# Two of eleven chunks of a feed forward product as seven block products, in four of five stages

## What is computed

```python
def swiglu(x, w_in, w_out):
    a, b = jnp.split(x @ w_in, 2, axis=-1)
    return (jax.nn.silu(a) * b) @ w_out

f = swiglu(rms_norm(h, g[0]), ffn1_w_in[l], ffn1_w_out[l])
h = h + FFN_RES * rms_norm(f, g[1])
...
ffn = jnp.dot(jax.nn.silu(jnp.dot(h2, w_ffn_gate)) * jnp.dot(h2, w_ffn_up), w_ffn_down)
```

## Time and profile before

| what | value |
|---|---|
| device time, median of 3 runs | 1419.55 us (1419.17 to 1420.1) |
| span of the profiled execution | 1417.5 us |
| median above that span | 2.05 us |
| PE busy | 1404.2 us, 99% |
| DVE busy | 940.8 us, 66% |
| ACT busy | 723.2 us, 51% |
| POOL busy | 150.7 us, 11% |
| weights and all else read from HBM | 280.70 MB |

### The profile page before, as it was taken

How to read it: one execution, slowest core, us unless ns; L and a number is a source line. 1 busy time by engine, 2 the same in 40 slices (tenths; PEclk the granted TensorE clock), 3 DMA queues, 4 the chain that set the end, 5 groups by cost and what they waited for, 6 DMA issues and landing times.

```text
span 1417.5 us, 19077 instructions
## 1 busy us (share of the span) xinstructions
PE 1404.2 (99%) x7339; PEld 1149.0 (81%) x7339; DVE 940.8 (66%) x1294; ACT 723.2 (51%) x1042; POOL 150.7 (11%) x232
## 2 busy tenths in 40 slices
PE   9999999999999999999999999999999999999998
PEld 7888888688888888888878888888877788888886
DVE  6666667886676667665786857755568666765544
ACT  6444455564443445543755645446556644654442
POOL 1600010010000000000172100000552110000000
PEclk9999999999999999999999999999999999999999
DMA  9686765256876778868544688763945355565551
GB/s 317 199 252 201 260 203 205 68 177 199 259 243 206 235 233 259 252 216 264 181 144 163 202 205 265 250 211 125 247 154 194 119 178 179 163 209 184 201 193 61
DMA packets 236346, 286.15 MB, mean 202 GB/s; under 512 B 37028, under 2 KB 160720, under 8 KB 236256
## 3 DMA queue, kind: packets, MB, share of 16 engines
q1 hardware_dynamic: 235856, 284.63, 63.1%
q10 hardware_dynamic: 400, 0.31, 0.1%
HBM read 280.70 MB, written 4.20 MB: 201 GB/s over the span
## 4 chain that ended last, share of the span: by engine, by line
PE 95%; DVE 2%; issue 1%; ACT 1%; DMA 0%; SPq 0%; POOL 0%; POOLq 0%; ACTq 0%
PE ps L583 30%; PE ps L586 29%; PE ps L584 29%; PE pst L790 1%; PE pst L949 1%; DVE wlo L475 1%; PE pst L1225 1%; PE ps L1172 0%; DMA raw<-in_ffn_w_in_dram 0%; ACT whi L466 0%; PE pst L1539 0%; PE pst L2112 0%; PE ps L1209 0%; PE ps L1689 0%; PE pst L2321 0%
## 5 line engine op out<-in xcount | busy, mean ns | idle before, releaser
L475 DVE TENSOR_TENSOR wlo<-raw,whi 128x1024 fp32r<-128x1024 f32 (+2 forms) x474 | 564.2, 1224 | 252.3 <-ACT whi L466 250.7
L466 ACT ACTIVATE whi<-raw 128x1024 fp32r<-128x1024 f32 (+2 forms) x474 | 472.3, 1040 | 233.7 <-PE ps L586 94.0
L583 PE MATMUL ps<-whi,xh 128*128 128x512 f32 (+2 forms) x1438 | 563.9, 392 | 1.8 <-ACT xh L829 0.8
L584 PE MATMUL ps<-wlo,xh 128*128 128x512 f32 (+2 forms) x1438 | 553.6, 385 | 0.0
L586 PE MATMUL ps<-whi,xl 128*128 128x512 f32 (+2 forms) x1438 | 545.1, 385 | 0.0
L583 PEld LDWEIGHTS ps<-whi,xh 128*128 128x128 f32 x1438 | 270.0, 188 | 61.9 <-issue 4.7
L586 PEld LDWEIGHTS ps<-whi,xl 128*128 128x128 f32 x1438 | 270.0, 188 | 54.9
L584 PEld LDWEIGHTS ps<-wlo,xh 128*128 128x128 f32 x1438 | 270.2, 188 | 51.0
L583 PE MATMUL ps<-whi,gh 128*128 128x512 f32 x440 | 172.0, 391 | 0.0
L584 PE MATMUL ps<-wlo,gh 128*128 128x512 f32 x440 | 171.2, 389 | 0.0
L586 PE MATMUL ps<-whi,gl 128*128 128x512 f32 x440 | 153.4, 389 | 0.0
(11 more groups left out here) (272 smaller groups left out, 894.2 us busy)
## 6 DMA issues: line engine op xcount, KB each, us to landing
raw<-in_ffn_w_in_dram SPq DMA_DIRECT2D x174, 512.0 KB, 5.4
raw<-in_ffn_w_out_dram SPq DMA_DIRECT2D x40, 1024.0 KB, 5.8
raw<-in_w_in_dram SPq DMA_DIRECT2D x26, 1024.0 KB, 5.1
adat<-in_w_ada_dram SPq DMA_DIRECT2D x96, 256.0 KB, 3.1
raw<-in_w_ffn_gate_dram SPq DMA_DIRECT2D x22, 512.0 KB, 4.1
raw<-in_w_ffn_up_dram SPq DMA_DIRECT2D x22, 512.0 KB, 5.1
raw<-in_hyb_w_in_dram SPq DMA_DIRECT2D x10, 1024.0 KB, 5.2
raw<-in_gla_w_in_dram SPq DMA_DIRECT2D x10, 1024.0 KB, 5.1
```

The lines of the kernel that those rows point to most:

```text
L466: e.activation(split_of(whi, j), raw_of(j), ACT.Copy).then_inc(*whi_made.up(j))
L475: e.tensor_tensor(split_of(wlo, j), raw_of(j), split_of(whi, j).bitcast(F32), ALU.subtract).then_inc(*wlo_made.up(j))
L583: e.matmul(ps[:, 0:n], a, whi_of(j, k), start=first and k == 0, stop=False)
L584: last = e.matmul(ps[:, 0:n], a, wlo_of(j, k), start=False, stop=False)
```

## The change

In stages 2, 3, 5 and 7, chunks 8 and 9 of the first product (x of 256x1024 by weights of 1024x1024: 512 columns of a and 512 of b) become one product of 2x2 blocks in Strassen's way (in Winograd's form): seven products of 128 rows by 512 by 512 columns in the place of eight. Each has one unit of weights and 12 matmuls. Sums of blocks of x are made and split once a stage (`sxh`, `sxl`). Sums of blocks of the weights are made by DMAs of POOL that add onto what lies in the buffer (`accum_op`), in `rowx` (both `rows`) and `workx` (`junk` and `xtmp`), but for one sum, which VectorE makes (`dve_t2`). P2 alone has its weights in the `raw` ring. Three results are copied out of their bank by ScalarE (`act_part`), two subtracted by VectorE (`dve_combine`). The seven stand one by one between the other chunks: 0, 1, P1, 2, P2, 3, P5, 4, P6, 5, P3, 6, P7, 7, P4, 10. Four banks are kept for them, and chunks from 2 on all use the same two banks. `ada_units` counts the products' units too: a stage has 37 units for 34. The loads of the gain vectors move to the first unit of the down product.

The core of the diff (left out: buffer declarations, the new index tables `JC`, `JP`, `JD` in the place of `J0[st] + 4 * c`, the calls of `pool_strassen(e, st)` behind the openings in POOL's program, and VectorE's loop, which mirrors ScalarE's: `dve_combine` after the fourth splits of chunks 5 and 7, `dve_sx` after the gates of chunk 1, `dve_sx_lo` after those of chunk 2, glo and the pair's gates in P4):

```diff
+    def next(self, name, *until, tile=None):
+        k = (self.n if tile is None else tile) % len(self.tiles)
+        self.n += tile is None
         self.freed = [s.at(*what) for s, *what in self.held[k]]
         self.held[k], self.place[name] = list(until), k
...
-            for c in range(11):
+        STRASSEN = (2, 3, 5, 7)
+        PAIR = 8
+        BLOCK = {"p1": ("x1", 0, 0), "p2": ("ring", 1, 0), "p5": ("x1", 0, 1), "p6": ("x1", None, None),
+                 "p3": ("x2", 1, 1), "p7": ("x2", 0, 1), "p4": ("x1", 1, 0)}
+        product_unit, home, chunk_unit, down_unit = {}, {}, {}, {}
+        def sequence(st):
+            if st in STRASSEN:
+                return (0, 1, "p1", 2, "p2", 3, "p5", 4, "p6", 5, "p3", 6, "p7", 7, "p4", 10)
+            return tuple(range(11))
...
+            if i in home:
+                return
+            s = ring_no[i] % NRAW
...
-                e.wait_ge(*(s_first.at(0) if u == 0 and k else s_raw[u % NRAW].at(u)))
+                if u not in home:
+                    e.wait_ge(*(s_first.at(0) if u == 0 and k else s_raw[ring_no[u] % NRAW].at(u)))
+                elif plan[u][0]:
+                    e.wait_ge(*(s_x1 if home[u] == "x1" else s_x2)[k // 2].at(u))
+                else:
+                    e.wait_ge(*summed.at(u, "t2"))
...
+                if j in sum_before:
+                    dve_t2(e, sum_before[j])
...
+        sum_before = {JP[st, "p6"] - 3: st for st in STRASSEN}
+        def dve_t2(e, st):
+            e.wait_ge(*wlo_made.at(last_sub[product_unit[st, "p5"]]))
+            for half in range(2):
+                e.wait_ge(*s_x2[half].at(product_unit[st, "p3"]))
+            e.tensor_tensor(rowx[:, :], rowx[:, :], workx[:, :], ALU.add).then_inc(*summed.up(product_unit[st, "p6"], "t2"))
...
+        def pool_strassen(e, st):
+            def split(name):
+                e.wait_ge(*wlo_made.at(last_sub[product_unit[st, name]]))
+            e.wait_ge(*f_scaled.at(st - 1, 1, 1))
+            pool_product(e, st, "p1", False)
+            split("p1")
+            pool_product(e, st, "p5", True)
+            e.wait_ge(*xlo_made.at(st, "sums"))
+            pool_product(e, st, "p3", False)
+            split("p6")
+            pool_product(e, st, "p4", True)
+            split("p3")
+            pool_product(e, st, "p7", True)
...
+        def dve_sx(e, st):
...
+            e.wait_ge(*squares.at(("h", st, 1), 1))
+            e.wait_ge(*xlo_made.at(st, 1, 3 if st == 7 else 1))
+            e.tensor_tensor(junk[:, :].rearrange("p (k n) -> p k n", k=8), whole(xh), whole(xl), ALU.add
+                            ).then_inc(*summed.up(st, "x", 0))
+            e.tensor_tensor(a22, a21, a22, ALU.subtract).then_inc(*summed.up(st, "x", "p5"))
+            e.wait_ge(*summed.at(st, "x", "p5"))
+            e.tensor_tensor(a21, a11, a21, ALU.subtract).then_inc(*summed.up(st, "x", "p7"))
+            e.wait_ge(*summed.at(st, "x", "p7"))
+            e.tensor_tensor(a11, a22, a11, ALU.subtract).then_inc(*summed.up(st, "x", "p6"))
+            e.wait_ge(*summed.at(st, "x", "p6"))
+            e.tensor_tensor(a12, a12, a11, ALU.add).then_inc(*summed.up(st, "x", "p3"))
+        def act_sx(e, st):
+            e.wait_ge(*summed.at(st, "x", "p3"))
+            e.activation(sxh[:, :], workx[:, :], ACT.Copy).then_inc(*xhi_made.up(st, "sums"))
+        def dve_sx_lo(e, st):
+            e.wait_ge(*xhi_made.at(st, "sums"))
+            e.tensor_tensor(sxl[:, :], workx[:, :], sxh[:, :].bitcast(F32), ALU.subtract).then_inc(*xlo_made.up(st, "sums"))
...
+        def pe_product(e, st, name, base):
+            bank, tile, first, until = {
+                "p1": ("a", 4, True, (silu_made, st, PAIR, 1)), "p2": ("b", None, False, None),
+                "p5": ("c", 5, True, (gated, st, PAIR, 1)), "p3": ("d", 3, False, (gated, st, PAIR, 0)),
+                "p6": ("a", None, False, None), "p7": ("a", None, False, None), "p4": ("a", None, False, None)}[name]
+            if tile is not None:
+                acc.next((st, bank), until, tile=base + tile)
+                for done in acc.freed:
+                    e.wait_ge(*done)
+            if name == "p1":
+                acc.next((st, "b"), (silu_made, st, PAIR, 0), tile=base + 2)
+                b_freed[st] = acc.freed
+            ps = acc.of(st, bank)
+            if name == "p5":
+                e.wait_ge(*xlo_made.at(st, "sums"))
+            if name == "p2":
+                e.wait_ge(*part_made.at(st, "p1"))
+            if name in ("p3", "p7"):
+                e.wait_ge(*summed.at(st, "c12"))
+            if name == "p4":
+                e.wait_ge(*summed.at(st, "c22"))
+            def block(z, sums, k):
+                if name in x_sums:
+                    o = x_sums[name] * 512 + k * P
+                    return sums[:, o:o + P]
+                return x_block(z, k + (0 if name == "p1" else 4), 1 if name == "p4" else 0)
+            for i in range(2):
+                j = JP[st, name] + i
+                e.wait_ge(*wlo_made.at(j))
+                for k in range(2):
+                    a, b = block(xh, sxh, 2 * i + k), block(xl, sxl, 2 * i + k)
+                    e.matmul(ps[:, :], a, whi_of(j, k), start=first and not i and not k, stop=False, skip_group_check=True)
+                    e.matmul(ps[:, :], a, wlo_of(j, k), start=False, stop=False, skip_group_check=True)
+                    last = e.matmul(ps[:, :], b, whi_of(j, k), start=False, stop=i == 1 and k == 1, skip_group_check=True)
+                last.then_inc(*mm[1].up(j))
+        def product_done(st, name):
...
+        def act_part(e, st, name):
+            e.wait_ge(*product_done(st, name))
+            if name == "p7":
+                e.wait_ge(*summed.at(st, "c12"))
+            if name == "p1":
+                for done in b_freed[st]:
+                    e.wait_ge(*done)
+            e.activation(acc.of(st, "b")[:, :] if name == "p1" else part[:, :], acc.of(st, "a")[:, :], ACT.Copy
+                         ).then_inc(*part_made.up(st, name))
+        def dve_combine(e, st, name):
+            e.wait_ge(*part_made.at(st, name))
+            d = acc.of(st, "d" if name == "p6" else "c")
+            e.tensor_tensor(d[:, :], acc.of(st, "c")[:, :], part[:, :], ALU.subtract
+                            ).then_inc(*summed.up(st, "c12" if name == "p6" else "c22"))
...
+        def act_silu_pair(e, st, tok):
+            e.wait_ge(*(product_done(st, "p4" if tok else "p2")))
+            if tok == 0:
+                e.wait_ge(*hid_turned.at(st, PAIR - 2))
+            e.activation(pair_of(hidx, tok, 256), both(acc.of(st, "ba"[tok])), ACT.Silu,
+                         scale=rstd(("h", st, tok)) if st < 7 else 1.0).then_inc(*silu_made.up(st, PAIR, tok))
+        def dve_gate_pair(e, st, tok):
+            e.wait_ge(*silu_made.at(st, PAIR, tok))
+            if tok == 0:
+                e.wait_ge(*product_done(st, "p3"))
+            e.scalar_tensor_tensor(pair_of(hidx, tok, 0), both(acc.of(st, "dc"[tok])),
+                                   rstd(("h", st, tok)) if st < 7 else 1.0, pair_of(hidx, tok, 256), ALU.mult, ALU.mult
+                                   ).then_inc(*gated.up(st, PAIR, tok))
...
-            for c in range(2, 11):
+            base = acc.n - 4
+            for c in sequence(st)[2:]:
+                if c in BLOCK:
+                    pe_product(e, st, c, base)
+                    if c == "p4":
+                        pe_hid_two(e, st, PAIR - 2)
+                    continue
                 def at(i, c=c):
-                    if c % 2 == 0 and i == 2:
+                    if c % 2 == 0 and i == (3 if st in STRASSEN and c == 10 else 2):
                         pe_hid_two(e, st, c - 2)
-                pe_chunk(e, st, j0 + 4 * c, readers[c], at)
+                pe_chunk(e, st, JC[st, c], readers[c], at, (base, base + 1) if st in STRASSEN else (None, None))
+            if st in STRASSEN:
+                acc.n += 4
...
+                if u == (down_unit[7] if 7 in STRASSEN else U0[7] + 4):
+                    load_row(e, "g5", gate_rows[1], D, [s_gates.at(5), gr_made.at(1, 1), *rows_free(7)])
+                for st in STRASSEN:
+                    if u == down_unit[st] and st in gains:
+                        load_row(e, st, gains[st], D, rows_free(st))
...
         def act_ffn(e, st, before):
...
+                        act_begin(e, JP[st, c] + i)
+                    if c == "p4":
+                        act_ghi(e, st, PAIR - 2)
+                        act_silu_pair(e, st, 0)
+                        act_silu_pair(e, st, 1)
+                    continue
                 for i in range(4):
-                    act_begin(e, j0 + 4 * c + i)
+                    act_begin(e, JC[st, c] + i)
+                    if st in STRASSEN and i == 2 and c in COMBINE:
+                        act_part(e, st, COMBINE[c])
```

(44 more changed lines are left out.)

112 lines of the change are left out of this document (81 added, 31 removed).

## The result

The changed kernel takes **1481.97 us** (median of 4 runs, 1476.77 to 1484.73; before in the same rounds 1419.36): ratio 1.0437, 95% interval 1.0424 to 1.0449, or +62 us. The forecast was 1446, its range ended at 1464: the direction is right, the size far too small. The profiled run is the fastest of the four, 1476.77 us with a span of 1474.9, 57.4 us over the span of before.

The account below looks back on a forecast made before the run. TensorE was taken to bound the kernel, busy 99% of the span. Stalls of 37.4 us less 10.9 us of removed matmuls gave +26.5 on the median 1419.55: 1446 us, own range 1433 to 1457, full range 1424 to 1464.

Parts of the forecast that it names:

- The mechanism and its spot: SyncE's queue: an ada load waiting for VectorE's ada add holds back weights behind a product; 14.3 us from gate to gate.
- the places of the waits: TensorE stalls at P2, T2, combines and plain gates: 9.4, 8.4, 13.3 and 6.3 us; none in stage 7.
- stage 3: Stalls forecast there at T2, P4's combine and the gates of chunks 5 and 7: 11.7 us lost.
- Rival 1: SyncE's queue, stages 2, 3 and 5: weights come before VectorE asks, all hidden, 1409 up to 1413 us; chance 0.11.
- VectorE's load: Added sums and splits take VectorE from 65.6 to about 84 us of a 93 us stretch: still under, if fed on time.
- the landing: Weights taken to reach ScalarE 5.88 us after issue; POOL's loads taken at 6 us, possibly twice that if they add.
- the forecast's own path for P3 in stage 2: P3 waits for a combine behind a late-loaded unit, a fold read and an ada sum: 5.1 us stall.
- The bound of 8.6 us for a landing: Weight loads of this stretch land in 4.1 to 8.6 us, median 5.4; a third at 8.6 adds 11 us.
- 37.4: TensorE's stalls in all, us: stage 2 loses 15.1, stage 3 11.7, stage 5 10.6, stage 7 nothing.
- 1433 and 1457: Ends of the forecast's own range: ten landings all at 4.1 us, or a third of them at 8.6 us.
- rival 2: TensorE's clock falls after the longer stalls, four costing 1.5 to 3 us more each: 1452 to 1458 us; chance 0.13.
- Rival 3: POOL's adding DMAs late, over 15 us a pair, stalling P7 and T2 in all four stages: 1460 to 1468 us; chance 0.10.

Follow-up runs that it names:

- run 1: Changed kernel with every ada tile's load two units later in SyncE's queue, nothing else: 1422.47 us, ratio 1.0018.
- run 5: Changed kernel with every ada tile's load one unit later in SyncE's queue: 1422.41 us, ratio 1.0016.
- run 7: Changed kernel with only the ada tiles at a product's place issued behind the weights of the next unit: 1439.69 us, ratio 1.0140.
- run 8: Changed kernel with all ada tiles one unit later except those at a product's place: 1473.37 us, ratio 1.0397.
- run 2: Kernel before the change with every ada tile's load two units later in SyncE's queue: 1419.59 us, ratio 0.9999.
- run 3: Changed kernel with the block products in stage 7 alone: 1417.45 us, ratio 0.9983.
- run 9: Changed kernel with P7's adding DMAs held until the weights of chunk 6's first unit have landed: 1475.22 us, ratio 1.0395.
- run 4: Changed kernel with POOL's adding DMAs made plain, same bytes and queue, those weight sums left out: 1466.77 us, ratio 1.0335.
- run 6: Changed kernel with matmuls of constants keeping TensorE busy ahead of P3 in stages 2 and 5: 1475.81 us, ratio 1.0393.
- run 10: Changed kernel with products in stages 3 and 7 alone and ada tiles two units later: 1418.22 us, ratio 0.9988.
- run 11: Changed kernel with products in stages 3, 5 and 7, ada tiles two units later, stage 5's gate rows loaded at unit 27 for 10: 1414.81 us, ratio 0.9963.
- run 12: Changed kernel, all four stages, ada tiles two units later, stage 5's gate rows loaded at unit 27 for 10: 1418.19 us, ratio 0.9992.

## Why the prediction was wrong in its size

**Right.** TensorE bound, and 12 matmuls a stage are 2.7 us (2.3 measured in stage 7). The mechanism and its spot are right: SyncE's order at the products (runs 1, 5, 7, 8), harmless before (2), absent in stage 7 (3). So are the places of the waits but one, and stage 3 within a microsecond (12.6 for 11.7), though partly by luck, as said above. Rival 1, all hidden at 1409, is what run 1 comes near to, within 13 us. VectorE's load did not bind (run 1 has all of it).

**Wrong, first: the landing.** "POOL's DMAs appear nowhere ... I take 6" priced their own lateness and not what they do to SyncE's weights. The forecast carried 5.88 us for the load at every stall, from a trace without a second queue. Beside adding DMAs it is 12.85 (P3, stage 2), 12.6 (the burst ahead of P3, stage 5) and 12.2 (chunk 2, stage 5). With the 7.0 us more, the forecast's own path for P3 in stage 2 gives 5.1 + 7.0 = 12.1 for 12.4 measured. In stage 5 the weights at 920.52 are there after 6.9 us (1.1 more, and not by adding DMAs, run 9), and the burst's first split starts at 917.08 where the path has 0.97 us behind the chunk's start at 912.75, 3.4 late: 4.1 + 1.1 + 3.4 = 8.6 for 8.5. The bound of 8.6 us for a landing lay below the values that came, because it was taken from the trace of before. These two stalls are 11.7 of the 13.6 us by which the idling passed 37.4. Run 4 shows the adding as such worth 15 us with what follows it. Some of the forecast's sums don't come out of their terms: the 5.1 of P3 in stage 2 is not written out, so its agreement proves little; 1433 and 1457 reckon a landing from the median of 5.4, and from the path's own 5.88 would be 1428 and 1455; VectorE's terms add up to 17.0 us, so 83 us and not 84. None of this reaches the 36 us that were missing.

**Wrong, second: the clock stood at nothing in the sum.** I gave rival 2 a chance of 0.13 as another way it could go, at 1.5 to 3 us for each of four long stalls. It happens with the stalls, not instead of them: six times, 13.5 us, or 2.2 each. The price of one was right; that it was 3 to 6 us at half clock no row of before told, and the stretches were 3.4 to 13.7 us, part of them still in the wait. Run 6 confirms that the cost is real. The rule of the Trainium skill (TensorE: Matmul & The Clock Gate, the HAM clock gate), that TensorE falls to half clock when idle and returns with work, is borne out here: granted clock 0.50 from 400.80, in the wait that began at 397.18, and matmuls 0.23 us apart again from 414.70 on. The clock belonged in the sum.

The books on the profiled span: 51.0 idling + 13.5 half clock - 10.9 matmuls + 3.8 beside these, mostly the edges of the waits, = 57.4. By the forecast's way, 37.4 + 13.6 + 13.5 explain all but those 3.8 and the 5 us by which the median stands above the profiled run. These 5 may be the wait ahead of chunk 4 in stage 2, 3 us shorter in this execution than in runs 4, 6 and 9, and the half clock that follows the longer one; that is not shown. **Rival 3** had the right culprit mostly in the wrong role. Its condition, over 15 us for a pair, was not met: POOL's adding DMAs landed after 13.1 us at most. In the kernel after, splits waited three times for adding DMAs, 4.2 us in all, and T2 once for P3's plain ones, 2.2 us in stage 5, with 1.0 us of TensorE's wait behind it. What cost most was the lateness of SyncE's weights beside them. The rival's figure, 1460 to 1468, was nearer than mine, but not for its reason. Only once the tiles are moved does T2's wait for POOL become one of the main stalls left (runs 10 to 12).

## What to carry to other kernels

When a change takes slack away, follow each queue of loads for the one whose wait now stands ahead of urgent weights. Moving the ada tiles one place was worth 60 us here; moving them two places gave nothing in the kernel before. Price a new DMA queue by what it does to the loads beside it, and an adding DMA above a plain one. A forecast wait of TensorE is to be summed together with the half clock behind it. No length of a wait tells safely whether it comes: 3.2 us in the kernel after and 2.5 in run 1 left the clock at full, while 2.1 us in run 12 and 2.8 in run 10 were followed by 3.4 us at half clock. And where one order is put right, the next late load comes out, here T2's.

## What the runs showed of the hardware

With adding DMAs in flight less is moved. Two windows with the DMA engines full show it, the first with P7's adding DMAs beside the weights (kernel after), the second in run 9 before those were issued (length, busy us and count of PE, PEld, DVE, ACT and POOL, clock, DMA share, GB/s):
```profile
398.00:400.00 2.00, 0.00 (x0) 0.00 (x0) 0.00 (x0) 0.00 (x0) 0.00 (x0) 1.00 1.11 239
```
```profile
400.00:402.00 2.00, 2.00 (x11) 1.65 (x10) 0.00 (x0) 0.00 (x0) 0.00 (x0) 1.00 1.07 367
```
The share (last but one) is full in both, and 239 GB/s are moved for 367. With plain DMAs in both queues it was 364 (run 4, 400 to 402). POOL's loads as a whole, adding and plain, land after a median of 8.0 us (18 of them, into `rows`) and 7.4 (12, into `work`) in the kernel after; with all plain, in run 4, after 6.2 and 5.4. The clock came back only some time after the work had: P3's twelve matmuls in stage 2 start 0.43 us apart to the last.
